# nsa attention with probabilities scaled before they are turned, products on halves of the array's columns, and branches summed in PSUM

## What is computed

```python
q, kc, vc, ks, vs, kw, vw, g_logits = jnp.split(h @ w_in, splits, axis=-1)
kcmp = compress(partial_rope(kv(kc), pos), cmp_pe[0], cmp_w1[0], cmp_w2[0])
vcmp = compress(kv(vc), cmp_pe[1], cmp_w1[1], cmp_w2[1])
...
p_c = masked_probs(s_c, cmp_end[None, :] <= qidx[:, None])
o_c = jnp.einsum('bgrqn,bngd->bqgrd', p_c, vcmp)
...
p_s = masked_probs(s_s, m_s)      # selected keys (ks, vs)
o_s = jnp.einsum('bgrqk,bgqkd->bqgrd', p_s, vsel)
...
p_w = masked_probs(s_w, m_w)      # keys of the window (kw, vw)
o_w = jnp.einsum('bgrqk,bkgd->bqgrd', p_w, vwc)
return gc[..., 0:1] * o_c + gc[..., 1:2] * o_s + gc[..., 2:3] * o_w
```

## Time and profile before

| | us |
|---|---|
| median of 3 runs (2884.45 to 2886.47) | 2885.82 |
| profiled execution | 2884.84 |
| its span | 2883.0 |
| PE busy | 2812.2 (98%) |
| DVE busy | 1860.1 (65%) |
| ACT busy | 1546.0 (54%) |
| POOL busy | 149.1 (5%) |
| nsa layer from its projections' end to its first output row | 1267.7 to 1350.8 |

### The profile page before, as it was taken

The page is one execution under the profiler, slowest core; times in us unless marked ns, Lnnn a source line. Parts: engine busy times, 40 slices in busy tenths (PEclk is TensorE's granted clock), DMA queues, the critical chain, the costliest instruction groups (busy, mean ns, idle before and its releaser), DMA issues.

```text
span 2883.0 us, 34918 instructions
## 1 busy us (share of the span) xinstructions
PE 2812.2 (98%) x13484; PEld 2303.9 (80%) x13484; DVE 1860.1 (65%) x2728; ACT 1546.0 (54%) x2656; POOL 149.1 (5%) x254
## 2 busy tenths in 40 slices
PE   9999999999999999999999999999999999999998
PEld 7887788888788888878888888788787788787786
DVE  6766776676566677646776766677654754645654
ACT  6546654655665465546655546665444444444442
POOL 1010100000000000000001001100100000000000
PEclk9999999999999999999999999999999999999999
DMA  8664467566446766642566675367663665653652
GB/s 261 223 229 161 141 218 248 183 223 222 161 154 217 243 190 229 215 150 70 187 232 219 216 260 186 103 208 242 229 212 135 200 189 189 227 190 132 190 190 88
DMA packets 358629, 559.41 MB, mean 194 GB/s; under 512 B 14624, under 2 KB 246048, under 8 KB 358208
## 3 DMA queue, kind: packets, MB, share of 16 engines
q1 hardware_dynamic: 350720, 535.02, 55.8%
q0 software_dynamic: 7600, 21.81, 2.2%
q10 hardware_dynamic: 144, 0.36, 0.0%
HBM read 556.03 MB, written 1.10 MB: 193 GB/s over the span
## 4 chain that ended last, share of the span: by engine, by line
PE 92%; DVE 5%; ACT 1%; issue 1%; POOL 1%; DMA 0%; DVEq 0%; ACTq 0%; POOLq 0%
PE ps L660 38%; PE ps L721 26%; PE ps L666 19%; PE ps L630 4%; PE ps L832 1%; PE ps L801 1%; DVE LO L1508 1%; POOL ST L2046 1%; DVE XL L1549 0%; DVE M L1626 0%; PE ps L809 0%; DVE M L1587 0%; PE ps L949 0%; DVE SB L1791 0%; ACT SB L1326 0%
## 5 line engine op out<-in xcount | busy, mean ns | idle before, releaser
L660 PE MATMUL ps<-HI,XH 128*128 128x512 f32 (+1 forms) x2496 | 984.1, 394 | 4.0 <-DVE LO L1508 1.4
L660 PE MATMUL ps<-LO,XH 128*128 128x512 f32 (+1 forms) x2496 | 971.4, 389 | 0.0
L1508 DVE TENSOR_TENSOR LO<-RAW,HI 128x1024 fp32r<-128x1024 f32 x468 | 567.6, 1223 | 335.7 <-ACT HI L1169 332.9
L666 PE MATMUL ps<-HI,XL 128*128 128x512 f32 (+1 forms) x2496 | 769.4, 389 | 0.4
L1513 DVE SCALAR_TENSOR_TENSOR LO<-RAW,GC,HI 128x512 fp32r<-128x512 f32 (+1 forms) x896 | 622.4, 744 | 189.1 <-ACT HI L1176 186.6
L1169 ACT ACTIVATE HI<-RAW 128x1024 fp32r<-128x1024 f32 x468 | 490.5, 1059 | 457.6 <-PE ps L721 286.6
L1176 ACT ACTIVATE HI<-RAW,GC 128x512 fp32r<-128x512 f32 (+1 forms) x896 | 588.1, 714 | 158.0 <-PE ps L666 133.0
L666 PEld LDWEIGHTS ps<-HI,XL 128*128 128x128 f32 x2496 | 466.7, 188 | 105.7 <-DVE XL L1549 7.9
L660 PEld LDWEIGHTS ps<-HI,XH 128*128 128x128 f32 x2496 | 469.9, 188 | 101.2 <-issue 2.4
L660 PEld LDWEIGHTS ps<-LO,XH 128*128 128x128 f32 x2496 | 470.1, 188 | 92.6
L721 PE MATMUL ps<-HI,AH 128*128 128x512 f32 x880 | 273.5, 392 | 0.0
(11 more groups left out here) (182 smaller groups left out, 1968.7 us busy)
## 6 DMA issues: line engine op xcount, KB each, us to landing
RAW<-in_ffn_w_in SPq DMA_DIRECT2D x350, 512.0 KB, 4.7
RAW<-in_ffn_w_out SPq DMA_DIRECT2D x88, 1024.0 KB, 5.0
RAW<-in_w_ada SPq DMA_DIRECT2D x48, 1024.0 KB, 5.1
RAW<-in_w_in SPq DMA_DIRECT2D x44, 1024.0 KB, 5.1
RAW<-in_w_ffn_in SPq DMA_DIRECT2D x88, 512.0 KB, 4.7
RAW<-in_diff_w_in SPq DMA_DIRECT2D x24, 1024.0 KB, 5.1
RAW<-in_w_ffn_out SPq DMA_DIRECT2D x22, 1024.0 KB, 4.9
RAW<-in_moba_w_in SPq DMA_DIRECT2D x12, 1024.0 KB, 5.1
```

The costliest lines, as they stand in the source:

```text
L660: e.matmul(ps[:, b + t, 0:nw], XH[:, k, t * P:(t + 1) * P], q[s][:, c * nw:(c + 1) * nw], start=(k == 0 and q is HI), stop=False)
L666: i = e.matmul(ps[:, b + t, 0:nw], XL[:, k, t * P:(t + 1) * P], HI[s][:, c * nw:(c + 1) * nw], start=False, stop=(k == 7))
L1508: e.tensor_tensor(LO[n % NSPLIT][:, 0:w], RAW[t.buf][:, at[1] * w:(at[1] + 1) * w], HI[n % NSPLIT][:, 0:w].bitcast(F32), ALU.subtract).the ...
```

## The change

- A unit is now a pair of heads in one branch with u // 2 the pair and u % 2 the branch, so the two branches of a pair follow each other.
- DVE makes CG (`weights`) directly after the exponentials, and GpSimd multiplies the probabilities in SB with it, in place, four `tensor_scalar` operations a unit. PE turns the scaled probabilities (`turned`).
- The copy of the turned probabilities out of PSUM is shared: ACT copies the first head (`first_head`), DVE the second (`second_head`); each is 128x384.
- The products have the values as the stationary operand and the turned probabilities as the moving one: for each head 256 and 128 columns, head 0 on the lower and head 1 on the upper half of the array's columns (`outputs_by_columns`). The result is rows by head dimension, columns by token, which is the form that XH and XL want. Both branches and the compressed one (`compressed`, one pair of 256 columns for each pair of heads) add up in one bank of PSUM. M, TP, their four additions and 16 turns are gone.
- XH and XL come from that bank for each pair (`pair_high`, `pair_low`).
- PE's loop turns unit u-1 and multiplies u-2 beside the scores of u+2, so it is one unit deeper. The scores of units 0 and 1 stand before and inside the compression. `clock` is gone from this layer.
- The whole softmax of the compressed branch stands before the loop on DVE, with the maxima of units 2 and 3 between its steps.
- Three of the eight splits of the output weights stand inside the loop (u = 9, 11, 13). Unit 15's products stand behind the first output rows.
- Tiles of the layer get other places in memory.

```diff
+            def outputs_by_columns(st, u, b, first, v):
+
+
+                PT = st.t["PT"]
+                for kt in range(2):
+                    for j in range(2):
+                        o = e.matmul(ps[64 * j:64 * j + 64, b, kt * P:S], v(kt),
+                                     PT[:, u % 2, j, 0:S] if kt == 0 else PT[:, u % 2, j, S:S + P],
+                                     start=(first and kt == 0), stop=False, skip_group_check=True)
+                o.then_inc(s_mix, 1)
...
+                def unit_scores(u):
+                    p = u // 2
+                    scores(st, u, lambda j, c0, w: QT[64 * j:64 * j + 64, p, c0:c0 + w],
+                           lambda j, c0, w: KSW[64 * j:64 * j + 64, u % 2, p // 2, c0:c0 + w], False, 2 * ((u + 1) % 2))
...
-                    return lambda j, kt: TM[:, kt, c0:c0 + 64]
-
+
+                e.wait_ge(s_cp, c["cp"] + 5)
+                e.wait_ge(s_tn, c["tn"] + 10)
+                unit_scores(0)
+                e.wait_ge(s_e, 8)
+                windows(0)
+                e.wait_ge(s_cp, c["cp"] + 6)
                 e.wait_ge(s_tn, c["tn"] + 12)
+                unit_scores(1)
+                windows(1)
                 e.wait_ge(s_hs, 2)
-                for i in range(2):
-                    scores(st, i, q_row(i), k_row(i))
 
...
-                def mixed(i):
-                    e.wait_ge(s_pt, c["pt"] + i + 1)
-                    if i >= 2:
-                        if i <= 9:
-                            e.wait_ge(s_o, c["o"] + i - 1)
-                        else:
-                            e.wait_ge(s_tp, tp_of(i - 2))
-                    outputs(st, i, x["PT"], i % 2, 6 + i % 2, 2, 64, value(i))
...
-                for i in range(16):
-                    if i + 2 < 16:
-                        e.wait_ge(s_ex, c["ex"] + i + 1)
-                        scores(st, i + 2, q_row(i + 2), k_row(i + 2))
-                    if i == 15:
-                        e.wait_ge(s_ex, c["ex"] + 16)
-                        outputs_flipped(st, 0, 16)
-                    e.wait_ge(s_ex, c["ex"] + i + 1)
-                    if i == 0:
+                def turned(u):
+
+                    SB = x["SB"]
+                    e.wait_ge(s_df, c["df"] + u + 1)
+                    if u == 0:
+
                         e.wait_ge(s_cm, 1)
-                    if i == 4:
+                    else:
+                        e.wait_ge(s_pt, c["pt"] + u)
+                        e.wait_ge(s_p1, c["p1"] + u)
+                    for j in range(2):
+                        o = turn(ps[:, (0 if u == 15 else 4) + j, :], [SB[:, u % 3, j, m * P:(m + 1) * P] for m in range(3)])
+                    o.then_inc(s_pf, 1)
+
+                def mixed(u):
+
+                    p = u // 2
+                    e.wait_ge(s_pt, c["pt"] + u + 1)
+                    e.wait_ge(s_p1, c["p1"] + u + 1)
+                    if u == 2:
+
                         e.wait_ge(s_cc, 2)
...
+                    outputs_by_columns(st, u, 6 + p % 2, u % 2 == 0, value(u))
+                    if u == 2:
+                        compressed(0)
+                    elif u % 2 == 1 and p >= 1:
+                        compressed(p)
+
+                def compressed(p):
+                    if p == 0:
+                        e.wait_ge(s_vb, 4)
+                    for j in range(2):
+                        o = e.matmul(ps[64 * j:64 * j + 64, 6 + p % 2, 0:S], VB[:, p // 2, (2 * p + j) % 4, :],
+                                     PTC[:, p // 2:8:4, :], start=False, stop=True, skip_group_check=True)
+                    o.then_inc(s_co, 1)
...
+                for u in range(17):
+                    if u + 2 < 16:
+                        e.wait_ge(s_ex, c["ex"] + u + 1)
+                        unit_scores(u + 2)
+                    if u >= 1:
+                        turned(u - 1)
+                    if u >= 2:
+                        mixed(u - 2)
+                    if u in (2, 3):
+                        compressed_turned(u - 2)
+
+                def ready(k, t):
+                    if (k, t) == (0, 0):
+
+                        e.wait_ge(s_pt, c["pt"] + 15)
+                        e.wait_ge(s_p1, c["p1"] + 15)
+                        e.wait_ge(s_ol, c["ol"] + 4)
+                    elif (k, t) == (0, 1):
+
+                        e.wait_ge(s_ol, c["ol"] + 8)
 
                 def hook(k, t):
-                    if (k, t) == (3, 0):
-                        outputs_flipped(st, 1, 20)
+                    if (k, t) == (0, 0):
+                        mixed(15)
                     last_hook(st, k, t, 8)
 
-                rows_of_outputs(st, st.w0 + 24, hook, s_end0)
+                rows_by(st.w0 + 24, lambda k, t: XH[:, k, t * P:(t + 1) * P], lambda k, t: XL[:, k, t * P:(t + 1) * P],
+                        8, [4, 4], ready, hook, s_end0)
 
...
+                e.wait_ge(s_e, 8)
+                for u in range(2):
+                    exps(st, u, 2 * ((u + 1) % 2))
                 for kv in range(2):
                     at = slice(64 * kv, 64 * kv + 60)
                     e.wait_ge(s_rawu, 3 + kv)
...
-                for i in range(16):
-                    if i == 15:
-                        outputs_high(st, 0)
-                    probs(st, i, 2)
-                    if i + 2 < 16:
...
+                def first_head(u):
+
+                    e.wait_ge(s_pf, c["pf"] + u + 1)
+                    if u >= 2:
+                        e.wait_ge(s_mix, c["mix"] + u - 1)
+                    e.activation(PT[:, u % 2, 0, :], ps[:, 0 if u == 15 else 4, 0:384], ACT.Copy).then_inc(s_pt, 1)
+
+                def pair_high(p):
+                    e.wait_ge(s_co, c["co"] + p + 1)
+                    e.activation(XH[:, p, :], ps[:, 6 + p % 2, 0:S], ACT.Copy).then_inc(s_oh, 1)
+
+                first_head(0)
+                for u in range(2, 18):
+                    if u < 16:
+                        exps(st, u, 2 * ((u + 1) % 2))
+                    if u >= 3:
+                        first_head(u - 2)
...
+                        pair_high(u // 2 - 3)
+                    if u in (9, 11, 13):
+                        split(st.w0 + 24 + (u - 7) // 2)
+                pair_high(6)
+                split(st.w0 + 30)
+                pair_high(7)
+                split(st.w1 + 2)
 
...
+                def weights(u):
+
+                    reciprocals(st, u)
+                    if u == 0:
+                        e.wait_ge(s_gs, 1)
+                    h0 = 2 * (u // 2)
+                    e.wait_ge(s_rc, c["rc"] + u + 1)
+                    e.tensor_tensor(CG[:, u], RC[:, u], GS[:, :, h0:h0 + 2, 1 + u % 2], ALU.mult).then_inc(s_cg, 1)
+
+                def second_head(u):
+
+                    e.wait_ge(s_pf, c["pf"] + u + 1)
+                    if u >= 2:
+                        e.wait_ge(s_mix, c["mix"] + u - 1)
+                    e.tensor_copy(PT[:, u % 2, 1, :], ps[:, 1 if u == 15 else 5, 0:384]).then_inc(s_p1, 1)
+
+                def pair_low(p):
+                    e.wait_ge(s_oh, c["oh"] + p + 1)
+                    e.tensor_tensor(XL[:, p, :], ps[:, 6 + p % 2, 0:S], XH[:, p, :].bitcast(F32), ALU.subtract
+                                    ).then_inc(s_ol, 1)
+
+                for u in range(2):
+                    maxima(st, u, 2 * ((u + 1) % 2))
+                for u in range(2):
+                    weights(u)
+
                 e.wait_ge(s_hs, 2)
                 e.memset(PC[:, :, :, :], 0.0).then_inc(s_z, 1)
...
-                def in_place(i):
-                    h0 = 2 * (i % 8)
-                    if i == 0:
-                        e.wait_ge(s_gs, 1)
-                    e.wait_ge(s_rc, c["rc"] + i + 1)
...
-                    got = ps[:, 6 + i % 2, 0:256].rearrange("p (t h d) -> p t h d", t=2, d=64)
-                    cg = CG[:, i].unsqueeze(3).to_broadcast([P, 2, 2, 64])
-                    e.wait_ge(s_cg, i + 1)
...
-                for i in range(16):
-                    reciprocals(st, i)
-                    if i == 15:
-                        outputs_low(st, 0)
-                    if i + 2 < 16:
-                        maxima(st, i + 2)
-                    if i >= 1:
-                        in_place(i - 1)
-                    compressed(i)
-                in_place(15)
-                outputs_out(st)
+                e.wait_ge(s_cm, 2)
+                e.tensor_tensor(pc, pc, MC[:, :, :].unsqueeze(3).to_broadcast([P, 2, 16, 15]), ALU.subtract
+                                ).then_inc(s_cm, 1)
+                maxima(st, 2, 2)
+                e.wait_ge(s_ce, 1)
+                e.tensor_reduce(SC[:, :, :], pc, AX.X, ALU.add).then_inc(s_cm, 1)
+                e.wait_ge(s_cm, 4)
+                e.reciprocal(CC[:, :, :], SC[:, :, :]).then_inc(s_cm, 1)
+                e.wait_ge(s_cm, 5)
+                e.tensor_tensor(CC[:, :, :], CC[:, :, :], GS[:, :, :, 0], ALU.mult).then_inc(s_cm, 1)
+                e.wait_ge(s_cm, 6)
```

(30 more changed lines are left out.)

159 lines of the change are left out of this document (47 added, 112 removed).

## The result

| | before | after |
|---|---|---|
| median of 4 runs each, us | 2886.14 (2884.45 to 2888.45) | 2918.7 (2916.58 to 2920.85) |
| span of the profiled execution | 2883.0 | 2919.0 |
| compression's start to first output row | 80.85 | 114.02 |

The changed kernel is slower: ratio 1.0112, interval 1.0095 to 1.013. The time is 32.6 us more, where 13 were forecast; it lies inside the range, near its upper end. The profiled execution (2920.85 us) was the slowest of the four, 2.2 us above their median; its span is 36.0 us longer than before.

What follows compares the result with a forecast made beforehand. PE bounds the kernel before; a ring of waits through PE and DVE was to bound the changed loop. 8.6 + 0.26 - 1.7 + 1 + 5.2 = +13.4 us on 2884.84 gives 2898.2, median 2899; range 2883 to 2920.

Steps and rivals of the forecast that it cites:

- ahead of the compression: Before the compression: unit 0's scores hide in PE's idle 2.2 us there, so no change.
- to unit 5's scores: From compressed scores' end to unit 5's scores: softmax, maxima, exponential, scores, copy, turn, products; 11.5 us at half clock.
- behind it: Behind the first output rows: unit 15's products and the last compressed pair (1.13 us), less 0.87 of turns; +0.26.
- The ring: PE's loop: turns wait for DVE's copy, queued behind maxima of scores just issued; 4.6 us an iteration, PE idle 1.9.
- The products: PE's output products by column halves, per unit: 0.70 us (0.64 to 0.88), for 1.29 before.
- The clock in the loop: Units' loop: PE's idle time brings clock falls; four half-clock stretches like the diff layer's 3.4 us, +5.2 us (0 to +33).
- the rival with a centre of 2914: Clock is half for much of the loop because PE idles in every iteration: 2908 to 2930 us; 15%.
- The start: Compression to compressed scores: ACT late, unit 0 and 1 scores moved, -1.7 us; half clock there 0 to +4.5, taken +1.
- The end: End of the loop: three iterations without scores, 4.5 us; output rows start without the 2.2 us of idle time.
- GpSimd: Four scalings a unit on GpSimd: 1.9 us (1.6 to 3), below the 4.6 us period, nothing on the path.
- PE bound, 2868: Rival: PE stays the bound with DVE's copy out in time, so its savings all count, some 17 us, 2868; 8%.
- DVE and GpSimd: Rival: DVE's last maxima instruction sits out one GpSimd scaling each iteration; ring 5.1 us, 5.5 later, 2904; 5%.

Runs made afterwards that it cites:

- e2: Changed kernel plus six constant products of 128 columns behind the scores of iterations 4 to 13, where PE is idle: 2901.6 us, ratio 1.006.
- e1: Changed kernel with DVE's copy of unit u-2's second head ahead of the maxima of unit u+2: 2886.83 us, ratio 1.0004 to the kernel before.
- e9: Changed kernel plus constant products in PE's two idle stretches at the start only: 2908.11 us, ratio 1.0079 to the kernel before.
- e15: Changed kernel with only each pair's copy and subtraction out of PSUM one iteration earlier: 2917.84 us, ratio 1.0108 to the kernel before.
- e7: e1 plus constant products in PE's two idle stretches at the start: 2880.94 us, ratio 0.9987 to the kernel before.
- e13: e1 with each pair's copy and subtraction out of PSUM one iteration earlier: 2886.22 us, ratio 0.9999 to the kernel before.
- e4: e1 with GpSimd scaling one element a unit in place of four blocks: 2884.90 us, ratio 0.9997 to the kernel before.

## Why the prediction was right, and where not

The forecast of each stretch beside the two traces, as a difference from before:

| stretch | forecast | after |
|---|---|---|
| ahead of the compression | 0 | +1.66 |
| compression to compressed scores | -0.7 | +2.23 |
| to unit 5's scores | -1.6 | -0.74 |
| units 5 to 15, ring | +12.3 | +13.6 |
| units 5 to 15, clock | +5.2 | +15.6 |
| to the first row | -2.0 | +2.53 |
| behind it | +0.26 | +1.17 |
| sum | +13.4 | +36.0 |

The ring and the clock in the ten iterations are told apart by e2. The forecast's +12.3 is ten of its eleven iterations (53.6 less 5.03) against 36.32.

- **The ring** was right, in place and size: idle time of 1.87 us for 1.9, released by DVE's copy, periods of 4.71 and 5.15 us at full clock (4.6 and 5.03). DVE's copy took 556 ns (0.55).
- **The products** take 0.80 us at full clock (in e1: 1319.10 less 1318.30), not 0.70, inside 0.64 to 0.88. Per unit 0.1 us more, and this is most of what the period was off.
- **The clock in the loop** is the step that failed. The forecast took four half stretches of 3.4 us, some 14 us in all, from the diff layer. The clock of 0.71 over 65.47 us means 38 us at half, and these cost 15.6 and not 5.2 (10.6 and 11.1 in the traces of e9 and e15, still twice the forecast). The mechanism was the right one, its size was not: the rival with a centre of 2914 had it. The diff layer was the wrong row to count by: there PE is busy for 16.31 of 19 us, in the ring for 46.70 of 65.47, and that with products that last longer at half clock. e2's row above, busy for 43.67 of 49.89 us at 1.00, is the one that resembles the diff layer.
- **The start.** The forecast said "0 to +4.5, I take +1" for the half clock between compression and compressed scores. It was there at once: two waits (1.56 and 0.51 us), then 12.1 us at 0.54. e7 and e9 put its price at 5.3 us (22.13 less 16.85), above the upper end; over all traces of this form it is some 4 (20.12 to 22.14 without constants, 16.85 to 18.05 with them), an estimate from their means. That ACT would be late was right: 1.56 us for Silu.
- **The end** of the loop was short by 2.6 us at full clock (e2: 12.10, for 9.5) and by 4.5 in the changed kernel, at 0.65. The forecast put the waits of the last iterations at nothing. At full clock, in e2, there are two:

```profile
1359.20 0.84 PE L629 MATMUL ps<-CST,SB 128*128 128x128 f32 x6 [0.84 <-DVE PT L1933]
...
1362.03 0.88 PE L629 MATMUL ps<-CST,SB 128*128 128x128 f32 x6 [0.75 <-POOL SB L2193]
```

The first is DVE's, which itself waited for ACT's last exponentials, and the second GpSimd's.
- **GpSimd**: 3.0 us a unit, at the upper bound, for 1.9. It is off the path in the ring, where it waited for its weights:

```profile
L2185 POOL TENSOR_SCALAR SB<-SB,CG 128x256 f32<-128x256 f32 x32 | 29.6, 924 | 0.0
L2185 POOL TENSOR_SCALAR SB<-SB,CG 128x128 f32<-128x128 f32 x32 | 19.3, 604 | 69.4 <-DVE CG L1918 69.3
```

- **PE bound, 2868**, was a rival that knew of one ring, and there are two. For ten of the sixteen units its 9.4 us are 5.9, and 4.9 at the 0.80 us that the products take. Without the first ring (e1) the ten iterations are 2.4 us shorter than before, because of the second; without both (e13) 4.8. More of its 17 us didn't come: in e13 the clock is 0.74 and 0.64 ahead of the loop, and the last iterations wait.
- **Ahead of the compression** the +1.66 isn't the change's: the compression starts anywhere between 1269.49 and 1272.64 us in the traces of the changed kernel's variants, whose code up to there is the same. Only the scores of unit 0 are new ahead of it, and they lie in an idle stretch.
- **DVE and GpSimd** didn't meet in the ring, as said there. NM's scaling took 170 ns on average, as in e4 without the scalings; in e1, where GpSimd works on beside the maxima, 243 (the changed kernel first, then e1):

```profile
L1785 DVE TENSOR_SCALAR NM<-MX 128x4 f32<-128x4 f32 x10 | 1.7, 170 | 0.3
```

```profile
L1785 DVE TENSOR_SCALAR NM<-MX 128x4 f32<-128x4 f32 x11 | 2.7, 243 | 0.4
```

## What to carry to other kernels

When an operation is moved to another engine, look at what stands ahead of it in that engine's queue in the same iteration: if that waits for something which the consumer issued just before, the two form a ring whose period has nothing to do with how busy the engines are; look for every such operation, since taking away one ring shows the next. Price the idle time that a ring puts on TensorE twice, once as it is and once for the clock: here the second was as large as the first. Where the wait can't be taken away, products that nobody reads, put into it, can be cheaper than idleness (17 us here). Put as a block of their own behind it they need not pay: `clock` cost 5.1 us and gave back 2.2. And look at more than one trace before pricing the clock, since it falls at different places in different executions of one kernel.
